# Expert weights loaded in long contiguous runs, with the transposes taking every 8th or 2nd column

## The chip, the cores and the metric

The kernel runs on one core of one Trainium2 chip. The metric is the device time of one execution in microseconds. Three executions of the kernel before took 1818.36, 1814.21 and 1817.06 us, median 1817.06 us.

## The reference

One encoder layer is applied to two requests, 512 and 256 tokens of width 1024, in f32: adaLN-modulated norm, a projection, neighbourhood attention and a bidirectional recurrence side by side, an output projection, then a mixture of experts, then a final norm. The change touches the mixture of experts alone:

```python
N_GROUPS = 4; EXPERTS_PER_GROUP = 8; N_EXPERTS = 32; EXPERT_HIDDEN = 512; TOP_K_IN_GROUP = 2

def hmoe(h, rg_w, rg_b, re_w, re_b, w1, w3, w2):
    # w1, w3: (32, 1024, 512), w2: (32, 512, 1024), f32
    # top-1 group of experts per token, then top-2 experts in that group
    ...
    def block_step(args):          # t: tokens of a block, e: its expert, wt: weights
        t, e, wt = args
        xb = hf[t]
        hid = jax.nn.silu(xb @ w1[e]) * (xb @ w3[e])
        return (hid @ w2[e]) * wt[:, None]
```

## The kernel before

The program is a chain of phases, each ended by a barrier of all engines: projections and attention, the recurrence, then (phase 5) output projection, second norm and router, then (phase 6) the experts, then (phase 7) the weighted sum of each token's two experts, the final norm and the store. The five engines run programs written by hand, and wait for each other by semaphores. The order within an engine is the order of the code.

In phase 6 every one of the 32 experts gets a block of 64 token slots (`BLK`); tokens beyond that would go to an overflow loop. Per expert:
- POOL gathers the 64 rows of 1024 features from `h2_dram` into `xg` (L1765), by an index list that SyncE has loaded six experts ahead (L1740).
- PE transposes them in 8 pieces of 128 features (`rows`, L1844): the piece of `xg` is the stationary operand, an identity the moving one. ACT copies the result to `xT`, whose piece j holds 128 features on the partitions (L1783).
- PE multiplies with w1 and w3 (L1857): 8 pieces of the contraction, two halves of 256 hidden columns each, which go to partitions 0 to 63 and 64 to 127 of the bank.
- ACT takes the SiLU of the first (L1790), DVE multiplies by the second into `hid` (L1823), PE transposes `hid` in two pieces (L1866), ACT copies them to `hidT` (L1796).
- PE multiplies with w2 (L1875): 4 pieces of the contraction, two halves of 512 output columns. DVE copies the result to `yb` (L1827), and two DMAs on ACT's queue store it (L1799).

The weights of an expert are 2 MB each for w1, w3 and w2. They lie in three slots (`w1_s`, `w3_s`, `w2_s`), so SyncE issues the load of expert e + 3 as soon as the same weight of expert e has been used (L1742 to L1744, in the order w1, w3, w2). Phase 5 already loads w1 and w3 of experts 0, 1, 2 and w2 of expert 2 (L1437, L1446, L1447); phase 6 begins with w2 of experts 0 and 1 (L1733). In a slot, partition p holds for each piece k of the contraction the weight row k * 128 + p:

```python
w1_v = A["exp_w1"][0].rearrange("e (k p) n -> e p k n", p=P)   # L1379, w3_v alike
w2_v = A["exp_w2"][0].rearrange("e (k p) n -> e p k n", p=P)   # L1381
```

A row of w1 is 512 f32, 2 KB; a row of w2 is 1024 f32, 4 KB. `view[e]` or `one(view, e)` picks an expert. The names of tensors in the trace: `in_exp_w` is any of the three weights, `h_scratch` is `h2_dram`, `slot_out` is `y_dram`, `arena` is the on-chip memory in which all tiles lie, `bank` is the accumulator memory.

Other loads that the rows below show: `w_out` in one DMA of 4 MB with rows of 4 KB (issued at L905), and the three bias tables of the attention, 1 MB each, 8 KB contiguous for each of 128 partitions (L328).

Of the kernel before, what the change touches and what calls it, by code (L numbers as in the profile page):

```python
# [28 lines left out]
P = 128  # L29
D = 1024  # L30
KD = D // P
# [16 lines left out]
BLK = 64  # L48
# [81 lines left out]
def build(nc, A, O, upto=6):  # L130
    ctx = ExitStack()
    with ctx:
# [4 lines left out]
        def sem(name):  # L137
            if name not in sems:
                sems[name] = nc.alloc_semaphore(name=name)
            return sems[name]  # L140
# [16 lines left out]
        bank = [banks[:, i * 512:(i + 1) * 512] for i in range(8)]  # L157
# [10 lines left out]
        ident = take(P)  # L168
# [1201 lines left out]
        NSLOT = 3  # L1370
        WEXP = 2 * KD * HID + KH * D
        w1_s, w3_s, w2_s = [], [], []
# [3 lines left out]
            w1_s.append(take(KD * HID).rearrange("p (k n) -> p k n", k=KD))  # L1376
            w3_s.append(take(KD * HID).rearrange("p (k n) -> p k n", k=KD))
        assert top[0] == base5
        w1_v = A["exp_w1"][0].rearrange("e (k p) n -> e p k n", p=P)  # L1379
        w3_v = A["exp_w3"][0].rearrange("e (k p) n -> e p k n", p=P)  # L1380
        w2_v = A["exp_w2"][0].rearrange("e (k p) n -> e p k n", p=P)  # L1381

        def one(ap, e):
            return ap[bass.ds(e, 1)].rearrange("o p k n -> p (o k) n")

        top[0] = ARENA - 2 * WEXP + KH * D
        wout = take(KD * D).rearrange("p (k n) -> p k n", k=KD)
# [34 lines left out]
        def sp_phase5(sp):  # L1422
            sp.wait_ge(sem("zero5"), 1)

            sp.dma_start(slot_dram.rearrange("(p n) o -> p (n o)", p=P), zero.bitcast(i32)[:, 0:NBLK * BLK // P]).then_inc(sem("slots_zero"), 16)
            for dst, src in ((sel5g, A["c_sel"][:, 0:2, :]), (before, A["c_before"]),
                             (ones, A["c_ones"]), (rw, A["router_w"]), (rb, A["router_b"].partition_broadcast(P)),
                             (expert_row, A["c_expert"]), (first_row, A["c_first"]), (fall_row, A["c_fall8"]),
                             (place, A["c_place"]), (token_i, A["c_token"])):
                sp.dma_start(dst, src).then_inc(sem("consts5_in"), 16)  # L1430
            for t in range(NT):
                sp.dma_start(x2[:, t, :], x_tile[t]).then_inc(sem("x5_in"), 16)

            unused = y_dram[NE * BLK:, :].rearrange("(p s) (j n) -> p (s j) n", p=P, n=512)
            sp.dma_start(unused, zero.unsqueeze(1).to_broadcast([P, MAX_OVER * BLK // P * 2, 512])).then_inc(sem("unused_zero"), 16)
            for slot, view in ((w1_s, w1_v), (w3_s, w3_v)):
                sp.dma_start(slot[0], view[0]).then_inc(sem("weights_in"), 16)  # L1437
            for t in range(NT):
                sp.wait_ge(sem("h2_ready"), t + 1)
                sp.dma_start(h2_dram[t * P:(t + 1) * P, :], h2[t % 2]).then_inc(sem(f"h2_out{t % 2}"), 16)  # L1440

            sp.wait_ge(sem("o5_mm"), 2 * NT)
            sp.wait_ge(sem("g2_mm"), 4)
            for k in (1, 2):
                for slot, view in ((w1_s, w1_v), (w3_s, w3_v)):
                    sp.dma_start(slot[k], view[k]).then_inc(sem("weights_in"), 16)  # L1446
            sp.dma_start(w2_s[2], w2_v[2]).then_inc(sem("weights_in"), 16)  # L1447
            sp.wait_ge(sem("list_ready"), 1)
            sp.dma_start(over_dram, lst_i[0:MAX_OVER, :]).then_inc(sem("list_out"), 16)
            sp.wait_ge(sem("weights_in"), 16 * 7)  # L1450
            sp.wait_ge(sem("list_out"), 16)
            sp.wait_ge(sem("unused_zero"), 16)
            sp.wait_ge(sem("h2_out0"), 48)
            sp.wait_ge(sem("h2_out1"), 48)
# [204 lines left out]
        xg = [take(D) for _ in range(2)]  # L1659
        xT = [take(KD * BLK).rearrange("p (k c) -> p k c", k=KD) for _ in range(2)]  # L1660
        sil, hid = take(HALF), take(HALF)
# [63 lines left out]
        def sp_phase6(sp):  # L1725

            for k in range(NSLOT):
                for name in ("h1_mm", "h3_mm") + (("y_mm6",) if k == 2 else ()):
                    sp.sem_inc(sem(f"{name}_w{k}"), 16)
            for k in range(LOOP):  # L1730
                sp.dma_start(idx_c[k][0:BLK, :], slot_dram[k * BLK:(k + 1) * BLK, :]).then_inc(sem(f"idx_in{k}"), 16)
            for k in range(2):
                sp.dma_start(w2_s[k], w2_v[k]).then_inc(sem(f"y_mm6_w{k}"), 16)  # L1733

            def ahead(c):

                static = isinstance(c.n, int)
                if not static or c.n + LOOP < NE:
                    sp.wait_ge(sem(f"xg_in{c.s}"), 16 * c.sn + 16)
                    sp.dma_start(idx_c[c.q][0:BLK, :], slot_dram[bass.ds(c.first_slot + LOOP * BLK, BLK), :]).then_inc(sem(f"idx_in{c.q}"), 16)  # L1740
                if not static or c.n + NSLOT < NE:
                    for name, slot, view in WEIGHTS:  # L1742
                        sp.wait_ge(sem(name), CREDIT + c.n + 1)
                        sp.dma_start(slot[c.w], one(view, c.e + NSLOT)).then_inc(sem(f"{name}_w{c.w}"), 16)  # L1744

            turns(sp, ahead, ahead=NSLOT)

            def over(c):
                sp.wait_ge(sem("over_y_out0"), 32 * c.n + 16)
                sp.dma_start(idx_o[0:BLK, :], slot_dram[bass.ds(c.first_slot, BLK), :]).then_inc(c.sem("idx_in0"), 16)  # L1750
                for name, slot, view in WEIGHTS:
                    sp.dma_start(slot[0], one(view, c.e)).then_inc(c.sem(f"{name}_w0"), 16)


            sp.wait_ge(sem("y_mm6"), CREDIT + NE)
            overflow(sp, over, with_expert=True)

        def pool_phase6(pool):
# [73 lines left out]
        def pe_phase6(pe):  # L1832
            for name in ("xT_mm", "h1_mm", "h3_mm", "hidT_mm", "y_mm6"):
                pe.sem_inc(sem(name), CREDIT)

            def rows(c):

                k = c.credit + c.n + 1
                pe.wait_ge(c.sem(f"xg_in{c.s}"), 16 * c.sn + 16)
                if not c.over:  # L1840
                    pe.wait_ge(sem("xT_ready"), k - 1)
                pe.sem_inc(sem("pe_turn"), 1)
                for j in range(KD):
                    ins = nc.tensor.transpose(bank[0][:, j * BLK:(j + 1) * BLK], xg[c.s][0:BLK, j * P:(j + 1) * P], ident[0:BLK, 0:BLK])  # L1844
                ins.then_inc(c.sem("xT_mm"), 1)

            def body(c, after=None):
                k = c.credit + c.n + 1
                pe.wait_ge(c.sem("xT_ready"), k)

                for name, slot, b, free in (("h1_mm", w1_s, 1, "sil_ready"), ("h3_mm", w3_s, 2, "hid_ready")):
                    pe.wait_ge(c.sem(f"{name}_w{c.w}"), 16 * c.wn + 16)
                    if not c.over:
                        pe.wait_ge(sem(free), k - 2)
                    for j in range(KD):
                        for n in range(2):
                            ins = nc.tensor.matmul(bank[b + 2 * c.s][BLK * n:BLK * n + BLK, 0:HALF], xT[c.s][:, j, :],  # L1857
                                                   slot[c.w][:, j, n * HALF:(n + 1) * HALF], start=(j == 0), stop=(j == KD - 1))
                    ins.then_inc(c.sem(name), 1)
                if after:  # L1860
                    rows(after)
                pe.wait_ge(c.sem("hid_ready"), k)
                if not c.over:
                    pe.wait_ge(sem("hidT_ready"), k - 1)
                for j in range(2):
                    ins = nc.tensor.transpose(bank[5][:, j * P:(j + 1) * P], hid[:, j * P:(j + 1) * P], ident)  # L1866
                ins.then_inc(c.sem("hidT_mm"), 1)

                pe.wait_ge(c.sem("hidT_ready"), k)
                pe.wait_ge(c.sem(f"y_mm6_w{c.w}"), 16 * c.wn + 16)  # L1870
                if not c.over:
                    pe.wait_ge(sem("y_ready6"), k - 2)
                for j in range(KH):
                    for n in range(2):
                        ins = nc.tensor.matmul(bank[6 + c.s][BLK * n:BLK * n + BLK, :], hidT[:, j % 2, j // 2, :],  # L1875
                                               w2_s[c.w][:, j, n * 512:(n + 1) * 512], start=(j == 0), stop=(j == KH - 1))
                ins.then_inc(c.sem("y_mm6"), 1)

            def over(c):
                rows(c)  # L1880
                body(c)

            rows(Main(0, 0, 0, 0, 0, 0))
            turns(pe, body, ahead=1, pairs=True)
            overflow(pe, over)

# [130 lines left out]
```

## Time and profile before

| What | us |
|---|---|
| median of three executions | 1817.06 |
| the profiled execution | 1818.64 |
| its span in the trace | 1816.9 |
| PE busy | 1437.8 (79%) |
| DVE, ACT, POOL busy | 623.9, 464.4, 297.5 |
| L1857 (w1, w3 matmuls), 2048 of them | 268.1 busy, 100.6 idle before them |
| L1875 (w2 matmuls), 512 of them | 116.9 busy, 19.1 idle before them |
| SyncE's DMA queue | 150636 packets, 295.42 MB |

The page averages over phases with different limits: PE's 79% comes mostly from the phases before 1200 us. The expert loop fills the stretch from about 1218 to 1760 us. "DMA share" is the mean share of time in which the core's 16 DMA engines had a packet under way; since packets of one engine overlap a little, it can exceed 1. "Idle before" is time in which the engine stood before instructions of a group, with what released it.

### The profile page before, as it was taken

What the parts mean: (1) busy time and instruction counts of PE and PEld (TensorE: products, weight loads), DVE (VectorE), ACT (ScalarE), POOL (GpSimd) and SP (SyncE); (2) the same over time, 40 slices, a digit from 0 to 9 for tenths busy, and PEclk for the clock granted to TensorE, in tenths of its full rate; (3) what the DMA queues carried; (4) which work ended last, traced back from release to release, by engine and by line L of the source; (5) the groups of instructions that cost most, each with busy time, mean ns of one, the idle gap of its engine ahead of it and who ended that gap; (6) DMA issues with size and microseconds to landing.
All of it is one profiled execution on the core that took longest, in us unless ns stands there. A gap on an engine that the chain in (4) does not pass through costs nothing. (4 is left out here: it accounts for less than half of the span.)

```text
span 1816.9 us, 22753 instructions
## 1 busy us (share of the span) xinstructions
PE 1437.8 (79%) x8896; PEld 878.3 (48%) x8896; DVE 623.9 (34%) x1044; ACT 464.4 (26%) x1072; POOL 297.5 (16%) x278
## 2 busy tenths in 40 slices
PE   5799999996629999999989689719877777777750
PEld 1445456654217777777767335405443434343420
DVE  0500044331756666666667632320000000000006
ACT  1201124432224455544546211101100000000003
POOL 0000023220562222122230510030000000000002
PEclk9799999998759999999999789759989998989995
DMA  6535441111341000100000372169999999999975
GB/s 226 180 121 186 152 138 47 47 36 50 112 167 36 19 19 22 33 18 19 19 1 2 109 261 85 69 245 371 376 380 376 386 378 386 378 385 377 385 284 194
DMA packets 161374, 321.22 MB, mean 177 GB/s; under 512 B 12544, under 2 KB 37248, under 8 KB 160908
## 3 DMA queue, kind: packets, MB, share of 16 engines
q1 hardware_dynamic: 150636, 295.42, 45.6%
q0 software_dynamic: 4672, 14.69, 2.7%
q10 hardware_dynamic: 5984, 9.97, 1.5%
q8 instruction: 57, 0.93, 0.2%
q14 instruction: 25, 0.20, 0.0%
HBM read 288.05 MB, written 32.00 MB: 176 GB/s over the span
## 5 line engine op out<-in xcount | busy, mean ns | idle before, releaser
L1207 PE MATMUL bank<-arena 128*128 128x128 f16 (+6 forms) x3696 | 434.7, 272 | 68.4 <-DMA arena<-direction_scratch 29.8
L1207 PEld LDWEIGHTS bank<-arena 128*128 128x128 f16 (+1 forms) x3696 | 336.6, 138 | 164.9 <-issue 99.0
L1857 PE MATMUL bank<-arena 128*64 128x256 f32 x2048 | 268.1, 422 | 100.6 <-DMA arena<-in_exp_w 63.8
L1857 PEld LDWEIGHTS bank<-arena 128*64 128x64 f32 x2048 | 165.9, 152 | 214.4 <-issue 88.4
L610 PE MATMUL bank<-arena 128*128 128x512 f32 x368 | 167.0, 601 | 0.7 <-ACT arena L359 0.7
L1043 ACT CAST arena<-bank 128x384 f16<-128x384 f32 x360 | 158.5, 482 | 15.9 <-PE bank L1207 11.1
L1823 DVE TENSOR_TENSOR arena<-bank,arena 128x256 f32<-128x256 f32 x32 | 13.6, 426 | 374.1 <-PE bank L1857 374.1
L1163 DVE CAST arena<-bank 128x384 f16<-128x384 f32 x216 | 116.8, 556 | 64.6 <-PE bank L1207 62.9
L1875 PE MATMUL bank<-arena 128*64 128x512 f32 x512 | 116.9, 598 | 19.1 <-ACT arena L1796 19.1
L347 POOL TENSOR_SCALAR arena<-arena 128x256 f32<-128x256 f32 (+1 forms) x64 | 51.9, 821 | 354.2 <-DVE arena L538 354.2
L610 PEld LDWEIGHTS bank<-arena 128*128 128x128 f32 x368 | 66.8, 189 | 85.2 <-issue 83.3
L1765 POOL DMA_INDIRECT arena<-h_scratch,arena x32 | 28.6, 894 | 467.4 <-PE bank L1844 442.3
L1617 PE MATMUL bank<-arena 128*128 128x512 f32 x192 | 86.8, 613 | 1.9 <-PEq L1966 1.9
L1144 DVE SCALAR_TENSOR_TENSOR arena<-bank,arena 128x512 f32<-128x512 f32 x96 | 65.1, 688 | 60.3 <-PE bank L1207 60.3
L617 PE MATMUL bank<-arena 128*128 128x256 f32 x368 | 84.4, 381 | 0.0
L1790 ACT ACTIVATE arena<-bank 128x256 f32<-128x256 f32 x32 | 12.3, 385 | 267.3 <-PE bank L1857 267.2
L617 PEld LDWEIGHTS bank<-arena 128*128 128x128 f32 x368 | 68.3, 189 | 16.0 <-issue 7.2
L1827 DVE COPY arena<-bank 128x512 f32<-128x512 f32 x32 | 22.2, 692 | 155.3 <-PE bank L1875 155.3
L511 DVE SCALAR_TENSOR_TENSOR arena<-bank,arena 128x511 f32<-128x511 f32 x15 | 11.2, 749 | 183.5 <-ACT arena L415 183.5
L1875 PEld LDWEIGHTS bank<-arena 128*64 128x64 f32 x512 | 34.4, 136 | 81.0 <-issue 54.4
L1783 ACT COPY arena<-bank 128x512 f32<-128x512 f32 x32 | 18.8, 587 | 209.9 <-PE bank L1844 209.9
L1617 PEld LDWEIGHTS bank<-arena 128*128 128x128 f32 x192 | 37.4, 197 | 48.4 <-issue 48.4
(238 smaller groups left out, 1422.6 us busy)
## 6 DMA issues: line engine op xcount, KB each, us to landing
arena<-in_exp_w SPq DMA_DIRECT2D x96, 2048.0 KB, 21.0
arena<-in_ada_w SPq DMA_DIRECT2D x12, 2048.0 KB
arena<-in_w_in SPq DMA_DIRECT2D x23, 512.0 KB, 4.3
direction_scratch<-arena SPq DMA_DIRECT2D x6, 1536.0 KB, 5.5
arena<-direction_scratch SPq DMA_DIRECT2D x12, 768.0 KB, 4.6
slot_out<-arena ACTq DMA_DIRECT2D x64, 128.0 KB, 5.7
slot_out<-arena SPq DMA_DIRECT2D x1, 6144.0 KB
arena<-in_x_sample SPq DMA_DIRECT2D x8, 512.0 KB, 4.8
```

The source lines that it names most:

```text
L347: nc.gpsimd.tensor_scalar(sc[p % NSC][0:nq, hh, 0:nk], sc[p % NSC][0:nq, hh, 0:nk], pinv[0:nq, 2 * p + hh:2 * p + hh + 1], None, ALU.mult) ...
L610: nc.tensor.matmul(bank[4 + i % 2], winb[i % NWIN][:, k, :], hTk[k][:, 0:T_S], start=(k == 0), stop=(k == KD - 1))
L617: ins = nc.tensor.matmul(bank[6][:, 0:T_P], winb[i % NWIN][:, k, :], hTk[k][:, T_S:TOK], start=(k == 0), stop=(k == KD - 1))
L1043: ins = nc.scalar.copy(inv[:, h, :], bank[4 + h % 4][:, 0:3 * P])
L1144: nc.vector.scalar_tensor_tensor(L, bank[4 + 2 * (j % 2) + k].rearrange("p (h c) -> p h c", h=2), BIG, seen[:, d, :].rearrange("p (h c) -> ...
L1163: ins = nc.vector.tensor_copy(inv[:, h, :], bank[4 + h % 4][:, 0:3 * P])
L1207: return nc.tensor.matmul(out, lhsT, r, start=start, stop=True, skip_group_check=True)
L1617: ins = nc.tensor.matmul(bank[2 + 2 * (t % 2) + hf], catT[:, k, t * P:(t + 1) * P], wout[:, k, hf * 512:hf * 512 + 512], start=(k == 0), s ...
L1765: nc.gpsimd.indirect_dma_start(xg[c.s][0:BLK, :], None, h2_dram, bass.IndirectOffsetOnAxis(ap=idx.bitcast(u32)[0:BLK, :], axis=0)).then_in ...
L1827: nc.vector.tensor_copy(yb[c.s], bank[6 + c.s]).then_inc(c.sem("y_ready6"), 1)
L1857: ins = nc.tensor.matmul(bank[b + 2 * c.s][BLK * n:BLK * n + BLK, 0:HALF], xT[c.s][:, j, :], slot[c.w][:, j, n * HALF:(n + 1) * HALF], sta ...
L1875: ins = nc.tensor.matmul(bank[6 + c.s][BLK * n:BLK * n + BLK, :], hidT[:, j % 2, j // 2, :], w2_s[c.w][:, j, n * 512:(n + 1) * 512], start ...
```

## The change

Each partition now holds consecutive rows of the weights. For w1 and w3, partition p holds rows 8p to 8p + 7, which are 16 KB contiguous in HBM. For w2, which is split into two halves h of 256 rows (the halves in which `hid` lies on the partitions), partition p holds rows 256h + 2p and 256h + 2p + 1, twice 8 KB. The slots keep their size and their place; `whole` views a slot with the same runs as the source, so that a DMA sees one long row for each partition (two for w2). Piece j of the contraction is now the rows 8p + j (2p + j in a half of w2), so the transposes must bring these features to partition p: they take every 8th column of `xg`, and every 2nd column of `hid`. The matmuls are as they were.

All instructions stay in number and order on all engines; only the access patterns of the DMAs on the weights and of the two transposes change.

```diff
-        w1_v = A["exp_w1"][0].rearrange("e (k p) n -> e p k n", p=P)
-        w3_v = A["exp_w3"][0].rearrange("e (k p) n -> e p k n", p=P)
-        w2_v = A["exp_w2"][0].rearrange("e (k p) n -> e p k n", p=P)
+        w1_v = A["exp_w1"][0].rearrange("e (p k) n -> e p (k n)", p=P)
+        w3_v = A["exp_w3"][0].rearrange("e (p k) n -> e p (k n)", p=P)
+        w2_v = A["exp_w2"][0].rearrange("e (h p j) n -> e p h (j n)", h=2, p=P)
 
         def one(ap, e):
-            return ap[bass.ds(e, 1)].rearrange("o p k n -> p (o k) n")
+
+            ap = ap[bass.ds(e, 1)]
+            return ap.rearrange("o p n -> p (o n)") if len(ap.shape) == 3 else ap.rearrange("o p h n -> p (o h) n")
+
+        def whole(slot):
+
+            return slot.rearrange("p k n -> p (k n)") if slot.shape[1] == KD else slot.rearrange("p (h j) n -> p h (j n)", h=2)
...
             for slot, view in ((w1_s, w1_v), (w3_s, w3_v)):
-                sp.dma_start(slot[0], view[0]).then_inc(sem("weights_in"), 16)
+                sp.dma_start(whole(slot[0]), view[0]).then_inc(sem("weights_in"), 16)
...
                     for name, slot, view in WEIGHTS:
                         sp.wait_ge(sem(name), CREDIT + c.n + 1)
-                        sp.dma_start(slot[c.w], one(view, c.e + NSLOT)).then_inc(sem(f"{name}_w{c.w}"), 16)
+                        sp.dma_start(whole(slot[c.w]), one(view, c.e + NSLOT)).then_inc(sem(f"{name}_w{c.w}"), 16)
...
                 for j in range(KD):
-                    ins = nc.tensor.transpose(bank[0][:, j * BLK:(j + 1) * BLK], xg[c.s][0:BLK, j * P:(j + 1) * P], ident[0:BLK, 0:BLK])
+                    ins = nc.tensor.transpose(bank[0][:, j * BLK:(j + 1) * BLK], xg[c.s].rearrange("s (c k) -> s k c", k=KD)[0:BLK, j, :], ident[0:BLK, 0:BLK])
...
                 for j in range(2):
-                    ins = nc.tensor.transpose(bank[5][:, j * P:(j + 1) * P], hid[:, j * P:(j + 1) * P], ident)
+                    ins = nc.tensor.transpose(bank[5][:, j * P:(j + 1) * P], hid.rearrange("s (c k) -> s k c", k=2)[:, j, :], ident)
```

The other loads of weights (L1446, L1447, L1733, and the overflow loop's L1752) get `whole` in the same way.

## Rows read from the trace of the kernel before

**Rows 1.** The page's slices of the whole span: DMA share in tenths, and GB/s.
```profile
DMA  6535441111341000100000372169999999999975
GB/s 226 180 121 186 152 138 47 47 36 50 112 167 36 19 19 22 33 18 19 19 1 2 109 261 85 69 245 371 376 380 376 386 378 386 378 385 377 385 284 194
```

**Rows 2.** A window: us, each engine's busy us, granted clock, DMA share, GB/s.
```profile
1300.00:1700.00 400.00, 298.56 (x2012) 160.43 (x2008) 24.61 (x44) 32.91 (x71) 19.63 (x22) 0.91 1.04 381
```

**Rows 3.** Waits, 1300 to 1740 us: engine, line, for whom; total, times, longest.
```profile
PE bank L1857 <- DMA arena<-in_exp_w: 61.6, 32, 3.6
```

**Rows 4.** Timeline of PE: start us, us, line, operation, count [idle before it].
```profile
1250.25 7.08 PE L1857 MATMUL bank<-arena 128*64 128x256 f32 x64
...
1262.40 7.08 PE L1857 MATMUL bank<-arena 128*64 128x256 f32 x64
...
1426.32 5.09 PE L1857 MATMUL bank<-arena 128*64 128x256 f32 x32 [2.96 <-issue]
...
1462.03 5.36 PE L1857 MATMUL bank<-arena 128*64 128x256 f32 x32 [3.03 <-DMA arena<-in_exp_w]
```

**Rows 5.** DMA issues, whole run: target, source, count, KB each, us to landing.
```profile
arena<-in_exp_w SPq DMA_DIRECT2D x96, 2048.0 KB, 21.0
...
slot_out<-arena ACTq DMA_DIRECT2D x64, 128.0 KB, 5.7
...
arena<-in_w_out SPq DMA_DIRECT2D x1, 4096.0 KB, 15.0
arena<-in_bias SPq DMA_DIRECT2D x3, 1024.0 KB, 8.2
...
arena<-h_scratch,arena POOLq DMA_INDIRECT x32, 6.7
```

**Rows 6.** Windows outside the loop: 8 KB, 4 KB and 2 KB runs.
```profile
228.00:232.00 4.00, 4.00 (x11) 1.81 (x11) 0.00 (x0) 0.00 (x0) 0.00 (x0) 1.00 1.01 426
1028.00:1036.00 8.00, 8.00 (x12) 2.83 (x12) 1.11 (x2) 3.51 (x6) 0.00 (x0) 0.67 1.02 416
1182.00:1197.00 15.00, 1.65 (x4) 1.14 (x4) 10.36 (x51) 0.00 (x0) 1.43 (x2) 0.50 1.05 389
```

**Rows 7.** Timeline of SyncE's queue: three places where loads are issued.
```profile
224.07 1.29 SPq L328 DMA_DIRECT2D arena<-in_bias  x3
...
1023.16 0.43 SPq L905 DMA_DIRECT2D arena<-in_w_out  x1
...
1174.91 10.62 SPq L1446 DMA_DIRECT2D arena<-in_exp_w  x4
```

**Rows 8.** Windows inside one expert's turn.
```profile
1448.00:1453.00 5.00, 2.92 (x28) 1.96 (x30) 0.00 (x0) 0.34 (x1) 0.00 (x0) 1.00 1.03 408
1453.00:1459.00 6.00, 5.43 (x34) 2.05 (x30) 0.43 (x1) 0.86 (x2) 0.90 (x1) 1.00 1.04 385
1442.00:1444.00 2.00, 0.00 (x0) 0.00 (x0) 0.00 (x0) 0.00 (x0) 0.00 (x0) 1.00 1.03 265
```

**Rows 9.** Windows around the start of the expert loop.
```profile
1200.00:1210.00 10.00, 0.00 (x0) 0.00 (x0) 0.00 (x0) 0.00 (x0) 7.56 (x9) 0.50 0.41 156
1224.00:1226.00 2.00, 2.00 (x10) 1.12 (x12) 0.00 (x0) 0.00 (x0) 0.66 (x1) 0.50 1.04 256
1230.00:1232.00 2.00, 2.00 (x22) 1.34 (x20) 0.00 (x0) 1.26 (x2) 0.00 (x0) 1.00 1.01 336
```

**Rows 10.** Timeline of POOL before the loop: the last scatter.
```profile
1209.41 0.95 POOL L1464 DMA_INDIRECT slot_token<-arena  x1 [0.30 <-issue]
```

**Rows 11.** The line of the row transposes: duration ns min/median/max.
```profile
L1844 PEld LDWEIGHTS bank<-arena x256: 134/138/226, 1221.9 to 1738.8; 64*128 64x128 f32 x128
```

**Rows 12.** Timeline of PE at the last expert.
```profile
1751.25 3.67 PE L1857 MATMUL bank<-arena 128*64 128x256 f32 x32 [2.21 <-DMA arena<-in_exp_w]
...
1756.41 3.65 PE L1875 MATMUL bank<-arena 128*64 128x512 f32 x16 [0.46 <-ACT arena L1796]
```

**Rows 13.** The page's count of DMA packets by size.
```profile
DMA packets 161374, 321.22 MB, mean 177 GB/s; under 512 B 12544, under 2 KB 37248, under 8 KB 160908
```

More of the change, by code:

```diff
@@ L1445, in sp_phase5 @@
                 for slot, view in ((w1_s, w1_v), (w3_s, w3_v)):
-                    sp.dma_start(slot[k], view[k]).then_inc(sem("weights_in"), 16)
-            sp.dma_start(w2_s[2], w2_v[2]).then_inc(sem("weights_in"), 16)
+                    sp.dma_start(whole(slot[k]), view[k]).then_inc(sem("weights_in"), 16)
+            sp.dma_start(whole(w2_s[2]), w2_v[2]).then_inc(sem("weights_in"), 16)
             sp.wait_ge(sem("list_ready"), 1)
@@ L1732, in sp_phase6 @@
             for k in range(2):
-                sp.dma_start(w2_s[k], w2_v[k]).then_inc(sem(f"y_mm6_w{k}"), 16)
+                sp.dma_start(whole(w2_s[k]), w2_v[k]).then_inc(sem(f"y_mm6_w{k}"), 16)
             def ahead(c):
@@ L1751, in over @@
                 for name, slot, view in WEIGHTS:
-                    sp.dma_start(slot[0], one(view, c.e)).then_inc(c.sem(f"{name}_w0"), 16)
+                    sp.dma_start(whole(slot[0]), one(view, c.e)).then_inc(c.sem(f"{name}_w0"), 16)
             sp.wait_ge(sem("y_mm6"), CREDIT + NE)
```

## The prediction

> **What bounds the kernel now.** I read the slices of the span first. From about 1226 to 1726 us (the 28th to the 38th of 40) the DMA row stands at 9 and the bytes moved stay between 371 and 386 GB/s [rows 1]. That is the expert loop, about 540 us of 1816.9. A window of 400 us inside it has a DMA share of 1.04 (all 16 engines hold a packet all the time, with some overlap), 381 GB/s, and PE busy for 298.6 of 400 us [rows 2]. The waits say the same from the other side: the matmuls of L1857 stood for the DMA of an expert weight 32 times between 1300 and 1740, 61.6 us [rows 3]. So one expert takes as long as its bytes take to arrive.
>
> The timeline gives both speeds. While the three experts loaded ahead last, PE repeats every 12.15 us (1250.25 to 1262.40). Later, from the first matmul of one expert (1426.32) to that of the second after it (1462.03), it is 35.71 us, so 17.855 us for one, with an idle of about 3 us before each [rows 4]. A weight lands 21.0 us (median) after its issue [rows 5], longer than an expert takes, so requests are always pending; what limits is how fast they are served. PE has 5.7 us per expert to spare.
>
> **What the change does to the transfers.** The bytes stay (2.097 MB for each of w1, w3, w2), the number of DMAs stays, no instruction changes its place on any engine. Only the length of the contiguous runs changes: w1 and w3 go from 1024 runs of 2 KB to 128 of 16 KB each, w2 from 512 of 4 KB to 256 of 8 KB. The price of a run length can be read from three stretches in which nearly one kind of transfer is under way and the DMA share is about 1 [rows 6] (which transfers these are is shown by the issues at 1175, 1023 and 224 us [rows 7]):
> - the weights w1, w3 loaded ahead, 2 KB runs, 1182 to 1197: 389 GB/s;
> - w_out, 4 KB runs, 1028 to 1036: 416 GB/s;
> - the bias tables, 8 KB runs contiguous in HBM, 228 to 232: 426 GB/s.
>
> The expert loop itself repeats the first two: 385 GB/s while w1 or w3 arrives, 408 while w2 does [rows 8]. Per run and engine (16 engines) this is 16 x 2048 / 389 = 84.2 ns, 16 x 4096 / 416 = 157.5 ns, 16 x 8192 / 426 = 307.7 ns. The last step is 150.2 ns for 4 KB more, so a run costs 75.1 ns per 2 KB and roughly 8 ns besides. A 16 KB run, which the trace has on no weight queue, extrapolates to 307.7 + 4 x 75.1 = 608 ns; a w1 is then 8 runs on each engine, 4.86 us (431 GB/s). One transfer takes 2.097 / 0.389 = 5.39 us with 2 KB runs, 5.04 with 4 KB, 4.92 with 8 KB.
>
> That the rate still rises above 358 GB/s is disputed by a page. The Trainium skill, "HBM Reference", section "Specifications (TRN2)", gives about 358 GB/s as a core's share of its HBM, and "DMA: Bandwidth & Descriptors", section "Specifications", puts the size from which a transfer runs at line rate at 512 B; by either the run length would be worth nothing from 2 KB up. The rows with 416 and 426 GB/s disagree with both for a core that runs alone.
>
> **The sum.**
> - w1 and w3, 29 of each in the loop (experts 3 to 31): 58 x (5.39 - 4.86) = 30.7 us less.
> - w2, 2 at the loop's start and 28 before the last w3: 30 x (5.04 - 4.92) = 3.6 us less. These count because the DMA share is 1.04 and 1.01 at 1224 and at 1230 [rows 9], so the engines go from the first w2 to w1 of expert 3 without a pause.
> - The rest of an expert's 17.855 us, 17.855 - 2 x 5.39 - 5.04 = 2.03 us, belongs to the gather of 64 rows (0.26 MB, landing in half the partitions), the two stores of 0.13 MB and the index list. I leave it alone. At the clean rates its bytes need 0.26/0.416 + 0.26/0.389 = 1.30 us, so 0.73 us is friction between queues (the stretch with 265 GB/s at share 1.03 [rows 8]). Its ends: it vanishes when there are fewer runs to alternate with, 28 x 0.73 = 20 us less; or it doubles, 20 us more.
> - The seven weights loaded ahead in the phase before the loop: nothing. That phase ends with the POOL scatters of L1464, the last of them issued at 1209.41 [rows 10], and the DMA engines run out of work before (share 0.41 from 1200 to 1210 [rows 9]). The cover is gone only if the weights landed some 5 us later.
> - Strided transposes. L1844 and L1866 load the data as the stationary operand, and their columns are now 32 and 8 bytes apart. A load takes 138 ns now [rows 11]; no row shows a strided f32 load, so I bound it from below by no change (a gain has no reason) and from above by four times as much, 0.41 us more each, ten per expert, 4.1 us. PE would then need 12.15 + 4.1 = 16.3 us per expert against the new arrival time of 17.855 - 2 x 0.53 - 0.12 = 16.7 us. So it is hidden at either end, except the two loads of L1866 behind the last expert's w3, which stand on the end path [rows 12]: 0 to 0.8 us. I take 0.3, near the unchanged row.
>
> The Trainium skill, "SBUF — State Buffer", section "Door 1: The DMA port swizzle" (its note on cachelines), says that accesses which cross a 16-byte line each time pay a penalty; by it L1844 (32 bytes) pays and L1866 (8 bytes) does not. No run of before shows either, and the sum would be the same but for the 0.3.
>
> After w3 of the last expert come its 3.67 us of matmuls, DVE, transposes, ACT, then L1875 at 1756.41 [rows 12]; w2, 4.92 us behind w3, is in time as it was. From there nothing changes.
>
> Sum: -30.7 - 3.6 + 0.3 = -34.0 us. The profiled execution took 1818.64 us (span 1816.9 and 1.7 around it), so 1784.6; it lay 1.6 us above the median of the three, so 1783. The period of the loop goes from 17.86 to about 16.7 us.
>
> **Rivals.**
> - Runs are cut. If the engines or the issue cut a long run into 4 KB pieces, w1 and w3 come at 5.04 us and w2 gains nothing: 58 x 0.35 = 20.3 us, 1797. Against it: 161374 - 160908 = 466 packets were 8 KB or larger [rows 13], and the three bias tables alone are 3 x 128 such rows. A milder kind, w1 and w3 no better than the 8 KB row, gives 58 x 0.47 + 3.6 = 31 us, 1786.
> - HBM is the limit, at the 389 GB/s that the longest stretch of weights shows: then the run length buys nothing and the time is 1817. The two figures of the Trainium skill quoted above lead here. The rows at 416 and 426 speak against it; for it only that they are short (8 and 4 us).
> - The other side: the rows' pitch. Before, the 128 partitions read neighbouring rows, 2 KB apart, in step; after, they read 16 KB apart. If such a pitch makes them meet in the same part of the memory, w1 and w3 slow down. It decides from below 389 GB/s. Priced with the worst full-share stretch near the loop, 256 GB/s [rows 9], a transfer takes 8.19 us: 58 x 2.8 = 162 us more, 1979; at 370 GB/s already 58 x 0.28 - 3.6 = 13 us more, 1830. Against it: pitches of 2, 4 and 8 KB in the three rows give a rising rate, none of it lost.
> - Small transfers starve. Gather and stores share the engines with runs of 608 ns instead of 84. The gather has 4 rows on each engine, a store pair 8; each row may wait for one long run, so 6.7 us to landing becomes some 9, and 5.7 becomes 10 [rows 5]. The gather's rows are used two experts later (about 33 us), a store buffer too. It costs only if the friction grows, the 20 us above: 1803.
> - PE takes over: from 0.45 us more per strided load. With eight times the load, 10 x 0.97 = 9.7 us, PE needs 21.9 us: 28 x 4 = 112 us more, 1930. Nothing speaks for a factor above 4.
>
> **Chances.** Forecast, with either price of the 16 KB run and friction moved by less than 10 us: 0.80, own range 1774 to 1793. Runs cut: 0.07 (1797). HBM limit: 0.03. Pitch: 0.04, a quarter of it too mild to see. Starving: 0.03 (1803, still faster). PE: 0.02. The rest, friction gone altogether (1763): 0.01. A difference under 0.2% (3.6 us) can't be told from none here. Faster: 0.91; same: 0.04; slower: 0.05. The range goes from 1768 (most of the friction gone) to 1800 (runs cut, or friction up).
>
> **What the profile after would show.** The weights' packets, 32 x 2560 = 82 thousand by the code, become 32 x 512 = 16 thousand; the loop runs at about 408 GB/s where it had 381, the starts of L1857 are 16.7 us apart, and the idle before them falls from 3 to 2 us; the w1 stretches reach about 430 GB/s. L1844's loads tell the price of the stride. The prediction is wrong if the rate in the loop stays near 381, if PE's idle on weights disappears, or if the rest of the period leaves 2.0 us.

## The result and the profile after

The changed kernel takes 1801.14 us (median of five, 1793.93 to 1803.11) against 1817.06 (1814.21 to 1819.46, five): ratio 0.9905, 95% interval 0.9878 to 0.9931, so 13 to 22 us saved. The forecast was 34 us saved. The direction is right and clear of noise; the size is half of the forecast. The range ended at 1800: the ratio puts the kernel at 1799.8, just inside, the bare median at 1801.14, just outside.

Below, the page's slices after, to be held against [rows 1], and its packet count against [rows 13].

```profile
DMA  6535441111341000100000254059999999999975
GB/s 228 182 117 194 143 149 48 48 36 32 132 169 36 19 19 19 30 25 19 19 1 1 98 191 170 36 233 332 371 401 393 399 401 387 402 386 395 400 296 186
DMA packets 95839, 321.22 MB, mean 179 GB/s; under 512 B 12545, under 2 KB 37249, under 8 KB 78989
```

The bytes are the same to the last digit; 65535 packets are gone (161374 to 95839), as the layout says to within one (32 x 2560 become 32 x 512). The loop still has the DMA engines at 9, and moves 386 to 402 GB/s where it moved 376 to 386.

Windows of the kernel after (us, busy us of PE, PEld, DVE, ACT, POOL, granted clock, DMA share, GB/s): weights loaded ahead, the end of the phase before the loop, the loop.

```profile
1184.00:1196.00 12.00, 0.00 (x0) 0.00 (x0) 9.37 (x46) 0.00 (x0) 1.30 (x2) 0.50 1.00 426
1200.00:1210.00 10.00, 0.00 (x0) 0.00 (x0) 0.00 (x0) 0.00 (x0) 7.37 (x8) 0.50 0.05 12
1300.00:1700.00 400.00, 315.78 (x2106) 174.28 (x2102) 26.42 (x47) 34.04 (x74) 20.53 (x23) 0.92 1.01 394
```

Alone on the queues, w1 and w3 now arrive at 426 GB/s; they arrived at 389 [rows 6]. The forecast had 431. In the loop, 381 [rows 2] became 394, not 408. A gain of 7.1% was forecast for the loop and 3.4% came, although w1 and w3 alone gained 9.5%: that is the question of this case. The phase before the loop gained nothing, as forecast: the DMA engines are idle there at 1200 (share 0.05, it was 0.41 [rows 9]) and the scatters of POOL set its end.

PE's timeline after (start, us, line, operation, count [idle before it]), to be held against [rows 4] and [rows 12]; L1863 is the old L1857, L1881 the old L1875.

```profile
1250.19 7.08 PE L1863 MATMUL bank<-arena 128*64 128x256 f32 x64
...
1262.73 3.62 PE L1863 MATMUL bank<-arena 128*64 128x256 f32 x32
...
1436.11 3.67 PE L1863 MATMUL bank<-arena 128*64 128x256 f32 x32
1442.63 5.05 PE L1863 MATMUL bank<-arena 128*64 128x256 f32 x32 [2.85 <-DMA arena<-in_exp_w]
...
1470.30 3.67 PE L1863 MATMUL bank<-arena 128*64 128x256 f32 x32
...
1733.12 3.67 PE L1863 MATMUL bank<-arena 128*64 128x256 f32 x32 [1.32 <-DMA arena<-in_exp_w]
...
1738.56 3.65 PE L1881 MATMUL bank<-arena 128*64 128x512 f32 x16 [0.68 <-ACT arena L1802]
```

PE with its weights present now repeats every 12.54 us (it was 12.15), with weights to wait for every 34.19 / 2 = 17.1 us (it was 17.86, and 16.7 was forecast). PE still waits for a weight, 28 times in 1300 to 1740. Some waits on either side carry no releaser ("issue"), so these lines of after and of before belong together with [rows 3]:

```profile
PE bank L1863 <- DMA arena<-in_exp_w: 71.5, 28, 3.2
PE bank L1863 <- issue: 8.0, 6, 1.8
```

```profile
PE bank L1857 <- issue: 34.2, 13, 3.2
```

In all 95.8 us of idle became 79.5 in the same 440 us, 3.9 us per expert 3.1. The single wait stayed near 3 us (2.85 above); the forecast had it fall to 2.

The matmuls on the loop's last w3 start 18.1 us earlier than in [rows 12] (1751.25 to 1733.12). The loop begins 0.6 us earlier (first L1857 at 1223.85, now L1863 at 1223.21), and what follows the last w3 takes 0.5 us longer (the span, 1816.9, became 1799.3). So the change lies in the arrival of weights in the loop.

Landing times, after (issues of the whole run; last column us from issue to landing), against [rows 5]:

```profile
arena<-in_exp_w SPq DMA_DIRECT2D x96, 2048.0 KB, 40.9
...
slot_out<-arena ACTq DMA_DIRECT2D x64, 128.0 KB, 8.0
...
arena<-h_scratch,arena POOLq DMA_INDIRECT x32, 9.4
```

A weight lands 40.9 us after its issue where it took 21.0. At three weights per 17.1 us that is some 7 on the way at once (an estimate), where it was 3 or 4. It goes with the number of runs (27.2 us with 4 KB runs and 33.5 with 8 KB, in runs_4k and runs_8k below), and by itself costs nothing: the fastest kernel below has 39.7. A gather takes 9.4 us instead of 6.7, a store 8.0 instead of 5.7.

The trace also records each packet by size and queue. Mean durations in ns for 1310 to 1660 us (of the recording's own clock, which runs 10.5 us ahead of the span's), with those of four experiments that are told below (a 4 KB packet of POOL's queue is the gather):

```
kernel            w1, w3 runs    w2 runs        gather   stores
before            2 KB:   92.0   4 KB: 163.3     229.1     84.9
after            16 KB:  664.8   8 KB: 329.0     210.5     84.2
nogather_before   2 KB:   88.7   4 KB: 162.9     169.4     84.5
nogather_after   16 KB:  616.1   8 KB: 311.8     161.2     84.1
pair_before       2 KB:   88.3   4 KB: 163.2     167.9     84.9
pair_after       16 KB:  615.4   8 KB: 311.6     160.5     84.2
```

A 16 KB run undisturbed takes 611 ns (median of the packets from 1190 to 1206; 608 was extrapolated). In the loop its mean is 665. The excess sits in the some 4 us in which a gather is under way: of the 853 runs of 16 KB that lie wholly inside a gather 99% are stretched, with a median of 867 ns and up to 1119. Beside the stores alone nothing is stretched (615).

### The profile page after: what moved, and what is told of

Same layout as the page of the kernel before. It is cut to its first block and busy times, and to the rows that moved or that the text cites. A ratio compares the mean times of both kernels' runs of the same rounds, so it can differ in the third digit from the quotient of the medians.

```text
span 1799.3 us, 22753 instructions
## 1 busy us (share of the span) xinstructions
PE 1440.2 (80%) x8896; PEld 888.4 (49%) x8896; DVE 624.3 (35%) x1044; ACT 464.0 (26%) x1072; POOL 298.0 (17%) x278
## 2 busy tenths in 40 slices
DMA packets 95839, 321.22 MB, mean 179 GB/s; under 512 B 12545, under 2 KB 37249, under 8 KB 78989
## 5 line engine op out<-in xcount | busy, mean ns | idle before, releaser
L1863 PE MATMUL bank<-arena 128*64 128x256 f32 x2048 | 263.3, 416 | 80.4 <-DMA arena<-in_exp_w 71.5
L1863 PEld LDWEIGHTS bank<-arena 128*64 128x64 f32 x2048 | 160.9, 151 | 191.9 <-DMA arena<-in_exp_w 84.4
L1881 PE MATMUL bank<-arena 128*64 128x512 f32 x512 | 116.9, 598 | 16.7 <-ACT arena L1802 16.7
L610 PEld LDWEIGHTS bank<-arena 128*128 128x128 f32 x368 | 66.8, 189 | 85.2 <-issue 83.3
L1833 DVE COPY arena<-bank 128x512 f32<-128x512 f32 x32 | 22.2, 693 | 165.6 <-PE bank L1881 165.6
L617 PEld LDWEIGHTS bank<-arena 128*128 128x128 f32 x368 | 68.3, 189 | 16.0 <-issue 7.2
L1881 PEld LDWEIGHTS bank<-arena 128*64 128x64 f32 x512 | 34.0, 136 | 77.5 <-issue 54.7
L1850 PE MATMUL bank<-arena 64*128 64x64 f32 x256 | 35.1, 278 | 37.6 <-DMA arena<-h_scratch,arena 37.6
## 6 DMA issues: line engine op xcount, KB each, us to landing
arena<-in_exp_w SPq DMA_DIRECT2D x96, 2048.0 KB, 40.9
```

The source lines that it names most:

```text
L610: nc.tensor.matmul(bank[4 + i % 2], winb[i % NWIN][:, k, :], hTk[k][:, 0:T_S], start=(k == 0), stop=(k == KD - 1))
L617: ins = nc.tensor.matmul(bank[6][:, 0:T_P], winb[i % NWIN][:, k, :], hTk[k][:, T_S:TOK], start=(k == 0), stop=(k == KD - 1))
```

## The experiments

Each ratio is to runs of the kernel before on the same chip. So that kernels timed on different chips can be compared, the last column applies the ratio to 1817.06 us.

| kernel | ratio, 95% interval | us at the base 1817.06 |
|---|---|---|
| after | 0.9905 (0.9878 to 0.9931) | 1799.8 |
| nogather_after | 0.9609 (0.9589 to 0.9629) | 1746.0 |
| nogather_before | 0.9817 (0.9797 to 0.9838) | 1783.8 |
| runs_8k | 0.9889 (0.9865 to 0.9912) | 1796.9 |
| runs_4k | 0.9903 (0.9879 to 0.9927) | 1799.4 |
| stride_only | 1.0000 (0.9987 to 1.0013) | 1817.1 |
| spread_8k | 0.9887 (0.9866 to 0.9908) | 1796.5 |
| halves_8k | 0.9900 (0.9871 to 0.9929) | 1798.9 |
| spread_2k | 1.0007 (0.9990 to 1.0023) | 1818.3 |
| distinct_after | 0.9904 (0.9871 to 0.9937) | 1799.6 |
| act_direct | 0.9918 (0.9889 to 0.9948) | 1802.2 |
| pair_after | 0.9696 (0.9676 to 0.9717) | 1761.8 |
| pair_before | 0.9885 (0.9865 to 0.9906) | 1796.2 |

**Is it the gather?** The first two take it out of either kernel.

```diff
-                nc.gpsimd.indirect_dma_start(xg[c.s][0:BLK, :], None, h2_dram,
-                                             bass.IndirectOffsetOnAxis(ap=idx.bitcast(u32)[0:BLK, :], axis=0))
+                nc.gpsimd.indirect_dma_start(xg[c.s][0:2, :], None, h2_dram,
+                                             bass.IndirectOffsetOnAxis(ap=idx.bitcast(u32)[0:2, :], axis=0))
```

nogather_after:

> The changed kernel with the gather cut from 64 rows to 2 per expert, so most of xg is stale: this leaves out the gather's transfers, nothing else. Theory A (the 64 rows that the gather lands in partitions 0 to 63 contend with the weights, and cost more when each of them alternates with a 16 KB run): without them the loop's period is 2 x 4.92 + 4.92 + 0.67 (stores) = 15.4 to 15.6 us instead of 17.2, time 1801 - 29 x 1.7 = about 1752. Theory B (the lost part of the gain lies with the stores or in the rate of the long runs themselves): the gather costs what its bytes cost, 0.26/0.416 = 0.63 us, period 16.5, time about 1782.

nogather_before:

> The kernel before with the same cut of the gather to 2 rows. Theory A: the gather cost 1.36 us here against 1.7 in the changed kernel, so period 17.86 - 1.36 = 16.5 us, time 1817 - 29 x 1.36 = about 1778, and the gap between the two kernels without gather is 25 to 30 us, close to the 31 that the run rates give. Theory B: the gap without gather stays at the 16 us that the full kernels show.

Measured: 1745.37 and 1782.82 us. Without the gather the two kernels lie 37.8 us apart (in the table's last column, to some 5 us; 25 to 30 was expected), with it 17.3. So the longer runs are worth all that was forecast, and the gather takes half of it back: it costs 33.3 us in the kernel before and 53.8 in the changed one. Its bytes, 4 packets per engine of 160 ns or 0.64 us per expert, would be 20. A window of each loop:

```profile
1300.00:1650.00 350.00, 288.36 (x2104) 163.97 (x2102) 25.73 (x46) 34.21 (x74) 19.55 (x23) 1.00 1.01 424
```

```profile
1300.00:1650.00 350.00, 278.82 (x1920) 151.80 (x1916) 23.92 (x43) 31.59 (x67) 17.85 (x21) 0.93 1.04 395
```

The first is nogather_after, the second nogather_before: 424 against 395 GB/s, 7% apart. The full kernels in the same window, after and then before, have 393 and 381:

```profile
1300.00:1650.00 350.00, 274.36 (x1836) 151.47 (x1832) 23.07 (x41) 30.47 (x65) 17.85 (x20) 0.92 1.01 393
```

```profile
1300.00:1650.00 350.00, 263.41 (x1779) 141.72 (x1776) 21.42 (x39) 29.51 (x62) 16.95 (x19) 0.91 1.04 381
```

Theory A holds and B falls.

**Does the price grow with the run?** runs_8k and runs_4k split w1 and w3 in two or four runs per partition:

```diff
-        w1_v = A["exp_w1"][0].rearrange("e (p k) n -> e p (k n)", p=P)
+        w1_v = A["exp_w1"][0].rearrange("e (h p j) n -> e p h (j n)", h=2, p=P)
...
-  xg[c.s].rearrange("s (c k) -> s k c", k=KD)[0:BLK, j, :]
+  xg[c.s].rearrange("s (h c j) -> s h j c", h=2, j=4)[0:BLK, j // 4, j % 4, :]
```

runs_8k:

> The changed kernel with w1 and w3 in two runs of 8 KB per partition instead of one of 16 KB (rows 512h + 4p + j; the transposes take every 4th column). A gather row then alternates with 309 ns instead of 611. Theory A, in the form that the gather's cost grows with the run beside it: period between 16.8 and 17.1 us, time 1790 to 1799, faster than the changed kernel although its runs are shorter. Theory C (the gather's cost does not depend on the run length, the rate of a 16 KB run is the 426 GB/s of an 8 KB run): period 17.2, time 1801 as the changed kernel.

runs_4k (h=4, j=2):

> w1 and w3 in four runs of 4 KB per partition, w2 in 8 KB, one gather as before. The gather cost 1.02 us beside 2 KB runs, 1.40 beside 8 KB, 1.58 beside 16 KB, so some 1.2 here. Period 15.64 + 2 x (5.04 - 4.92) + 1.2 = 17.1 us, time about 1796, level with the 8 KB kernel and a little faster than the 16 KB one (both theories; a check that the two effects offset each other).

Measured: 1793.77 and 1797.38 us. 4, 8 and 16 KB can't be told apart (0.9903, 0.9889, 0.9905, each to about 0.0025). That fits a gather that gets dearer as the runs get cheaper; it doesn't prove it, since runs_8k lies within the error of the changed kernel.

**Is it the stride?** stride_only has the two transposes of the changed kernel and the old layout of the weights (so it computes something else, at the same work).

> The kernel before with the strided transposes of the changed kernel alone; the weights keep the old layout, so features meet the wrong weight rows (output not the reference's). Both theories: time as before, 1817 (within 2 us), because PE waits for weights; PE's repeat while the weights loaded ahead last goes from 12.15 to 12.54 us (loads of L1844 at 202 ns instead of 138). If the stride were what ate the gain, the time would go up by 29 x 0.4 = 12 us or more.

Measured: 1815.47 us, ratio 1.0000. Its loads of L1844, and PE's repeat on weights already there:

```profile
L1844 PEld LDWEIGHTS bank<-arena x256: 182/202/212, 1222.6 to 1741.9; 64*128 64x128 f32 x128
```

```profile
1251.75 7.08 PE L1857 MATMUL bank<-arena 128*64 128x256 f32 x64
...
1264.29 1.90 PE L1857 MATMUL bank<-arena 128*64 128x256 f32 x16
```

202 ns instead of 138 [rows 11], 12.54 us instead of 12.15: the stride costs PE 0.39 us per expert and the kernel nothing. The rival in which PE takes over is excluded.

**Why is the gather dear?** Its 64 rows land in partitions 0 to 63. The first attempt, on the kernel with 8 KB runs (spread_8k) and on the kernel before (spread_2k), moved half of every row to the upper partitions, in a second gather (and to tell this from the split alone, halves_8k leaves both in the lower ones):

```diff
-        h2_dram = dram("h2_scratch", [TOK, D])
+        h2_dram = [dram(f"h2_scratch{h}", [TOK, W]) for h in range(2)]
...
-                nc.gpsimd.indirect_dma_start(xg[c.s][0:BLK, :], None, h2_dram,
+                for h in range(2):
+                    nc.gpsimd.indirect_dma_start(xg[c.s][h * BLK:(h + 1) * BLK, :], None, h2_dram[h],
```

spread_8k:

> w1 and w3 in runs of 8 KB (two per partition), and the gather spread over all partitions: features 0 to 511 of the 64 rows land in partitions 0 to 63, features 512 to 1023 in partitions 64 to 127, by two gathers of 2 KB rows; four full transposes instead of eight of half height. Theory P (the gather costs more than its bytes because all its rows land in the lower 64 partitions, whose weights arrive at the same time): it falls to the time of its bytes, 128 x 84 ns / 16 = 0.67 us, period 15.64 + 0.67 = 16.3 us, time about 1773. Theory Q (each gather row that alternates with a long run costs something, wherever it lands): twice as many rows, the gather costs 1.4 us or more as in the 8 KB kernel, period 17.0 or more, time 1794 to 1810.

halves_8k:

> The same two gathers of 2 KB rows, but both into partitions 0 to 63, with the transposes of the 8 KB kernel. Theory P: the gather costs 1.4 us as in the 8 KB kernel, period 17.0, time about 1794 (within 4). Theory Q: twice the rows cost up to twice the friction, 0.67 + 2 x 0.76 = 2.2 us, period 17.8, time about 1815.

spread_2k:

> The kernel before (2 KB runs, contiguous transposes) with the gather spread over all partitions. Theory P: the gather's cost falls from 1.02 to 0.67 us, period 17.5, time about 1805. Theory Q: no gain, 1815 or more.

Measured: 1795.22, 1799.26 and 1817.05 us. The spread gains nothing in either layout, so theory P falls as it was stated. halves_8k lies 5 us above P's 1794 and far below Q's 1815, but Q was not really tried: POOL's queue put two rows of 2 KB in one packet of 4 KB, so the number of gather packets stayed at 64 per expert. What halves_8k does show is that twice as many gather DMAs cost little or nothing (0.9900 against 0.9889 of runs_8k).

Next, the two things that set this gather apart from a plain load: what it reads, and who issues it. Each is one run; both give every expert the same 64 rows, so their output is not the layer's.

```diff
-  sp.dma_start(idx_c[k][0:BLK, :], slot_dram[k * BLK:(k + 1) * BLK, :])
+  sp.dma_start(idx_c[k][0:BLK, :], A["c_token"][0:BLK, 0:1], allow_slow_non_contiguous=True)
```

distinct_after:

> The changed kernel with the gather's index lists replaced by the constant tokens 0 to 63, loaded from an input (so every expert works on the same 64 rows). In the original lists the unused slots of a block (on average 64 - 1536/32 = 16 of 64) all name token 0, so one row of 4 KB is read many times at once. Theory D (these repeated reads are what makes the gather dear): the gather falls to its bytes, 0.64 us, period 15.6 + 0.64 = 16.25 us, time about 1770. Theory S (a gather from POOL's queue is dear by itself, whatever it reads): period 17.2, time about 1798 to 1801.

```diff
                 nc.scalar.copy(xT[c.s], bank[0].rearrange("p (k c) -> p k c", k=KD)).then_inc(c.sem("xT_ready"), 1)
+                if not c.over:
+                    act.dma_start(xg[c.s][0:BLK, :], h2_dram[0:BLK, :]).then_inc(sem(f"xg_in{c.s}"), 16)
```

act_direct:

> The changed kernel with each gather replaced by a plain load of rows 0 to 63 (same 64 rows of 4 KB into the same partitions 0 to 63), issued on ACT's queue; the index loads are left out. Theory S (POOL's queue and its descriptors are the cost): period 15.6 + 0.64 = 16.25 us, time about 1770, while distinct_after stays at 1798 or more. Theory D: the same 1770, but distinct_after too. Theory P2 (any 4 KB rows landing in the lower partitions beside long runs cost this, whatever the queue): 17.2 us, time about 1799, in both.

Measured: 1799.43 and 1799.40 us, both as the changed kernel. Neither the repeated token 0 nor the indirect DMA nor POOL's queue is the cause. 64 rows of 4 KB into partitions 0 to 63 cost the same as a plain load from ACT's queue (P2). The stores, also on ACT's queue and in 2 KB packets, are not stretched, but they read the on-chip memory and write HBM.

That left one reading of P: not how many bytes a half of the partitions gets in all, but which engine writes where within one DMA. On this reading all 16 engines carry a DMA over 64 partitions, into half of the partitions at a time, also in spread_8k, only one half after the other. So the last pair of runs gathers 128 rows, those of two experts, in one DMA over all partitions:

```diff
-                nc.gpsimd.indirect_dma_start(xg[c.s][0:BLK, :], None, h2_dram,
-                                             bass.IndirectOffsetOnAxis(ap=idx.bitcast(u32)[0:BLK, :], axis=0))
+                nc.gpsimd.indirect_dma_start(xg[c.q // 2][0:rows, :], None, h2_dram,      # rows = 128, even experts only
+                                             bass.IndirectOffsetOnAxis(ap=idx.bitcast(u32)[0:rows, :], axis=0))
...
+                half = slice(c.s * BLK, c.s * BLK + BLK)
-  xg[c.s].rearrange("s (c k) -> s k c", k=KD)[0:BLK, j, :], ident[0:BLK, 0:BLK]
+  xg[c.q // 2].rearrange("s (c k) -> s k c", k=KD)[half, j, :], ident[half, half]
```

pair_after:

> The changed kernel with one gather of 128 rows for two experts instead of one of 64 rows for each: the rows of the even expert land in partitions 0 to 63, those of the odd one in 64 to 127, in one DMA (three buffers of a pair; the transposes of an odd expert read the upper partitions; nothing is left out). Bytes and rows of 4 KB per expert stay. Theory R (in a DMA over 64 partitions all 16 engines write into the lower partitions, where half of the engines have their own weights to write; in one over all 128 each engine writes where its weights go): the gather costs its bytes, 0.64 us per expert instead of 1.58, period 15.6 + 0.64 = 16.25 us, time about 1770. Theory Q2 (four 4 KB rows per engine beside long runs cost this wherever they land): period 17.2, time 1799.

pair_before:

> The kernel before (2 KB and 4 KB runs) with the same gather for two experts. Theory R: gather 0.64 us instead of 1.02, period 16.84 + 0.64 = 17.5 us, time about 1804; the gap to pair_after is then 34 us, all of what the run lengths are worth. Theory Q2: 17.86, time 1815, and the gap stays 17 us.

Measured: 1764.12 us and 1795.46 us, for R's 1770 and 1804. pair_after is the fastest kernel of this case that leaves nothing out, 3% below the kernel before. In the table's last column the pair lies 34.4 us apart, twice the gap of the full kernels. Loop windows of pair_after and of pair_before:

```profile
1300.00:1650.00 350.00, 288.87 (x2034) 162.59 (x2034) 25.68 (x46) 33.41 (x72) 11.24 (x12) 0.97 1.01 425
```

```profile
1300.00:1650.00 350.00, 263.13 (x1844) 142.93 (x1838) 23.30 (x42) 29.94 (x66) 9.36 (x10) 0.95 1.04 396
```

For contrast, spread_8k, with as many bytes in either half of the partitions:

```profile
1300.00:1650.00 350.00, 269.00 (x1775) 146.92 (x1770) 22.82 (x41) 31.70 (x67) 36.15 (x41) 0.93 1.02 397
```

The landing times of pair_after's gathers and stores:

```profile
arena<-h_scratch,arena POOLq DMA_INDIRECT x16, 10.9
...
slot_out<-arena ACTq DMA_DIRECT2D x64, 128.0 KB, 8.0
```

The stores land as late as in the changed kernel, so a late landing was not the price. 425 GB/s with the gather is as much as 424 without it. The gather now costs 15.8 us (1761.8 - 1746.0) beside long runs and 12.4 beside short ones, not above what its bytes cost. The packet records account for it. From after to pair_after, per expert and engine: 16 runs of w1 and w3 shorter by 664.8 - 615.4 = 49 ns, 16 runs of w2 by 17.4, 4 gather packets by 50: 0.79 + 0.28 + 0.20 = 1.27 us, times 29 experts 37 us; measured 1799.8 - 1761.8 = 38.0. From before to pair_before: 128 x 3.7 + 4 x 61 = 0.72 us, times 29 some 21 us; measured 20.9. The friction is 17 us larger beside the long runs, and 17 us is what the change fell short of the forecast.

The pair differs from the single gather in more than its width: it has half as many gathers and index loads, and three buffers for two experts each where there were two for one each. The number of DMAs is not the cause: nogather_after issues all 32 gathers and lists, of 2 rows each, and moves 424 GB/s, and halves_8k doubles them at no clear cost. The deeper buffering, which lets a gather be issued earlier, was not tried by itself; against it stands that the packets themselves became shorter (a gather's 210.5 to 160.5 ns, a 16 KB run's 664.8 to 615.4).

## Why the prediction was half right

- **The bound** was read rightly: the loop goes at the rate of the weights, in both kernels, and every other part of the span stayed.
- **The price of a run** was right. 608 ns was extrapolated and 611 found; the rate of 16 KB runs is 426 GB/s instead of 431, which takes 58 x (4.92 - 4.86) = 3.5 us from the 30.7 and leaves 30.5 of the 34.0. The gaps with the gather cut (37.8 us) and with the gather paired (34.4), each to some 5 us, hold the forecast 34.0.
- **The step that failed** is the third line of the sum: the rest of an expert's turn, "I leave it alone". It put the change of this term at nothing, with bounds of 20 us less or 20 us more, and the cost went towards the upper one: by the runs without gather the gather's cost rose from 33.3 to 53.8 us, 20.5 more; by the paired gather it rose by 38.0 - 20.9 = 17.1 more (both to some 7 us). 34.0 less 3.5, less 17.1 or 20.5, is 13 or 10; the measured gain is 17.3 (12.5 to 22.2 by its interval). That 37.8 - 20.5 is 17.3 shows nothing, since 20.5 was got from the same four times. By the period the whole line grew less, from 2.03 to 17.1 - 3 x 4.92 = 2.3 us, some 9 us over 29 experts. So the stores and lists in that line may have become cheaper beside long runs; no run separates them.
- Why that line was mis-sized: I put the friction of 0.73 us down to alternation between queues, as a thing of the number of packets, and left it constant. The rows gave a hint: 265 GB/s at a DMA share of 1.03 [rows 8] means engines that hold packets and move them slowly, which a count of alternations does not explain.
- **The range held by its edge, not by its centre.** The story given 0.80 had its own range, 1774 to 1793, and missed. That 1799.8 lies under 1800 is owed to bounds that had been set for cut runs or for friction that doubles. Of the three signs of being wrong one came: the rest of the period left 2.0 us.
- **The rivals.** Starving small transfers had the right place, the right landing time for the gather (9 forecast, 9.4 found; stores 10 and 8.0) and nearly the right price, 1803 (1799.8 found), with a chance of 0.03. What was wrong was its condition, a wait for one long run per row: pair_after has the same rows beside the same runs, and its gathers, of twice the rows, land in 10.9 us, at no cost beyond their bytes. The cut runs are refuted by the packet sizes (65535 fewer), the limit at 389 GB/s and the pitch of 16 KB by the 426 GB/s, PE by stride_only.
- **Strided loads**: 64 ns more each for L1850 (202 instead of 138), 67 for L1872 (206 instead of 139), within the bound of four times. On the end path L1881 starts 5.44 us after the start of the last w3's matmuls, where L1875 started 5.16 us after it [rows 12]: 0.28 us, where 0.3 was put; the two loads are 0.13 of it. The Trainium skill's note on cachelines ("SBUF — State Buffer", "Door 1: The DMA port swizzle") would have only the 32 byte step pay; here the 8 byte step pays as much.
- **The two figures quoted**: I read the 358 GB/s of the Trainium skill ("HBM Reference", "Specifications (TRN2)") as a limit of this core. It is a core's share while both cores of a pair stream; the same section of the Trainium skill gives about 425 GB/s for a core that streams alone, and the 426 measured here agree with that. The Trainium skill's 512 B ("DMA: Bandwidth & Descriptors", "Specifications") are a least size for line rate, and above them the rate here still rose, from 389 GB/s with runs of 2 KB to 426 with 16 KB.

Shown by runs: that the gather eats the gain, that its cost does not depend on its indices, its queue or its being indirect, and that one DMA of 128 rows for two experts removes what exceeds its bytes. That the width is what does it in this pair rests on the shorter packets and on the failed rivals. Argued only: the way it happens, engines that write outside their own part of the memory. The Trainium skill has the map for it: in "DMA: Bandwidth & Descriptors", section "The descriptor swizzle", a DMA over 128 partitions has each engine write through one port of its own, and by "SBUF — State Buffer", "Door 1", partitions 0 to 63 reach 8 of the 16 ports. The contrast of spread_8k (397 GB/s, though runs of 8 KB alone also move 426 [rows 6]) and pair_after (425) agrees; no record here names an engine or a port. Nor does the reading say why 99% of the 16 KB runs inside a gather are stretched, and not only those of the engines that it has sharing a port. Why the gather's cost grows with the run beside it stays open too.

## What to carry to other kernels

When a loop is bound by DMA, price every stream in it, not only the one that changes: a small transfer over half the partitions can cost more than twice its bytes, and it can cost more once the large stream has got better (33 us here, then 54). Compare the rate of a clean stretch with that of the loop; here 389 (2 KB runs) and 416 (4 KB) against 381 hid a gather that cost 33 us, and removing it in both kernels showed it. Give such a transfer all 128 partitions in one DMA, for instance by fetching for two steps at a time.

## What was not expected of the hardware

- A load of 64 rows of 4 KB over partitions 0 to 63 stretches the weight packets beside it (16 KB: 615 to 665 ns in the mean, a median of 867 ns inside it), whether it is gathered by POOL or plainly loaded by ACT (669 ns); one of 128 rows over all partitions does not (615).
- Two DMAs of 64 partitions, one after the other in the two halves, are no substitute for one of 128: 8 KB runs of 330 ns in the mean in spread_8k against 312 in pair_after.
- A strided f32 load of the stationary operand costs the same 64 to 67 ns more for a step of 8 bytes as for one of 32.
